# One wait slot per pair of column blocks and per token half, instead of one per block, in a six-layer transformer kernel on one Trainium2 core

## The reference

```python
for i in range(DEPTH):                       # 4 layers
    h = mixer_a / mixer_b / mixer_c (x)      # qkv = x @ w_qkv; attention of 16 heads; @ w_o
    x = layer_norm(DN_ALPHA * x + h, ...)
    x = layer_norm(DN_ALPHA * x + swiglu(x, w_gate_up[i], w_down[i]), ...)
for layer in range(DEPTH_2):                 # 2 layers
    proj = rmsnorm(x) @ w_in[layer]
    y_a = chunked_spatial_gating(...)
    y_b = mamba2_mixer(...)                  # state space scan in chunks of 128
    y_c = diff_attention(...)                # 4 heads, two softmaxes each; rmsnorm of the output
    merged = g0 * (y_a @ w_branch_a) + g1 * (y_b @ w_branch_b) + g2 * (y_c @ w_branch_c)
    x = x + merged @ w_out[layer]
    up = causal_dwconv(rmsnorm(x) @ ffn_w_up, ...)
    x = x + (silu(gate) * val) @ ffn_w_down
```

## Time and profile before

| | |
|---|---|
| median of 3 runs | 2586.41 us (2585.18 to 2586.76) |
| the profiled execution | 2585.18 us, its span 2583.4 us |
| PE busy | 2454.9 us, 95% of the span |
| DVE, ACT, POOL busy | 1477.3, 1324.3, 480.9 us |
| TensorE clock granted, mean | 0.969 of full |
| the chain that ended last | PE 82%, DVE 8%, ACT 5%, issue 3% |
| moved from and to memory | 398.94 MB, 154 GB/s |

### The profile page before, as it was taken

One profiled execution on the slowest core, in us unless ns is written; L12 is line 12 of the kernel. 1 busy time (PEld: TensorE's weight loads), 2 busy tenths in 40 slices (PEclk: granted clock), 3 DMA queues, 4 the chain that ended last, 5 costly groups with the idle time before them and its releaser, 6 DMA issues.

```text
span 2583.4 us, 36889 instructions
## 1 busy us (share of the span) xinstructions
PE 2454.9 (95%) x15388; PEld 2162.7 (84%) x15388; DVE 1477.3 (57%) x2114; ACT 1324.3 (51%) x1974; POOL 480.9 (19%) x370
## 2 busy tenths in 40 slices
PE   7999999999899998999989989999999999899999
PEld 5689977777699776998769979889899898798898
DVE  5455454544654545555555456656676666566766
ACT  4454455554544555544445446546565565465654
POOL 3230041322400223101410001342100004421000
PEclk9799999999899999999889999999999989999999
DMA  6145543333355433554315544334445443344453
GB/s 243 49 176 183 184 158 114 115 115 130 114 194 182 164 132 132 193 186 175 132 66 196 183 160 156 126 143 147 166 176 182 179 155 123 132 156 169 165 194 131
DMA packets 58182, 398.94 MB, mean 154 GB/s; under 512 B 6816, under 2 KB 7072, under 8 KB 11680
## 3 DMA queue, kind: packets, MB, share of 16 engines
q1 hardware_dynamic: 56864, 393.75, 41.9%
q10 hardware_dynamic: 1152, 2.83, 0.3%
HBM read 395.51 MB, written 1.05 MB: 154 GB/s over the span
## 4 chain that ended last, share of the span: by engine, by line
PE 82%; DVE 8%; ACT 5%; issue 3%; POOL 1%; DMA 0%; SPq 0%; DVEq 0%; ACTq 0%; POOLq 0%
PE b L1139 12%; PE b L1141 12%; PE b L1140 12%; PE b L1073 12%; PE b L1074 11%; PE b L1075 11%; PE b L1078 8%; PE b L1082 4%; DVE wlo L1780 2%; ACT whi L1415 2%; DVE xl L1792 1%; ACT full L1411 1%; DVE st L1843 1%; DVE xn L1841 1%; DVE xn L1854 0%
## 5 line engine op out<-in xcount | busy, mean ns | idle before, releaser
L1780 DVE TENSOR_TENSOR wlo<-raw,whi 128x2048 fp32r<-128x2048 f32 x351 | 823.0, 2348 | 441.6 <-ACT whi L1415 441.4
L1415 ACT ACTIVATE whi<-raw 128x2048 fp32r<-128x2048 f32 x362 | 690.8, 1910 | 356.4 <-PE b L1141 225.6
L1139 PE MATMUL b<-xh,whi 128*128 128x256 f32 x2560 | 728.7, 285 | 0.0
L1141 PE MATMUL b<-xh,wlo 128*128 128x256 f32 x2560 | 722.8, 282 | 0.0
L1140 PE MATMUL b<-xl,whi 128*128 128x256 f32 x2560 | 722.8, 282 | 0.0
L1139 PEld LDWEIGHTS b<-xh,whi 128*128 128x128 f32 x2560 | 486.5, 190 | 8.1 <-issue 6.1
L1140 PEld LDWEIGHTS b<-xl,whi 128*128 128x128 f32 x2560 | 486.7, 190 | 1.9
L1141 PEld LDWEIGHTS b<-xh,wlo 128*128 128x128 f32 x2560 | 486.2, 190 | 0.0
L1073 PE MATMUL b<-whi,xh 128*128 128x512 f32 x832 | 356.0, 428 | 54.4 <-issue 38.0
L1074 PE MATMUL b<-wlo,xh 128*128 128x512 f32 x832 | 337.3, 405 | 0.0
L1075 PE MATMUL b<-whi,xl 128*128 128x512 f32 x832 | 336.8, 405 | 0.0
(11 more groups left out here) (225 smaller groups left out, 2896.3 us busy)
## 6 DMA issues: line engine op xcount, KB each, us to landing
raw<-in_w SPq DMA_DIRECT2D x362, 1024.0 KB, 4.8
gt<-in_rows SPq DMA_DIRECT2D x8, 512.0 KB, 3.9
bt<-in_rows SPq DMA_DIRECT2D x8, 512.0 KB, 4.8
abq<-in_rows ACTq DMA_DIRECT2D x2, 768.0 KB, 4.7
x<-in_x SPq DMA_DIRECT2D x1, 1024.0 KB, 6.3
bc<-in_rows SPq DMA_DIRECT2D x4, 256.0 KB, 5.0
out<-x SPq DMA_DIRECT2D x4, 256.0 KB, 2.1
msk<-in_masks SPq DMA_DIRECT2D x1, 768.0 KB, 7.8
```

Source lines behind the costliest of these rows:

```text
L1139: pe.matmul(out, wh[:, k, cs], ah[:, kk, :], start=kk == 0 and s == 0, stop=False, skip_group_check=True)
L1141: last = pe.matmul(out, wl[:, k, cs], ah[:, kk, :], start=False, stop=final and k == 3, skip_group_check=True)
L1415: return ac.activation(out, i, ACT.Copy)
L1780: ve.tensor_tensor(B.wlo[s][:, :], B.raw[r][:, :], B.whi[s][:, :], ALU.subtract).then_inc(sem["loV"], 1)
```

## The change

In `col_out` the inner loop over the two column blocks of a pair and its yield are gone: one `col` step now emits both blocks (24 matmuls), and there is one yield behind it. In `row_acc` (the branch without a boundary) the yield moves out of the loop over k: one yield per token half. A `col` tile and a `row` tile now have two yields in place of four. `tok_out` and the boundary branch are as before. The number of matmuls, their order within a tile, and the semaphore counts are the same. 

```diff
--- before.py
+++ after.py
@@ -313,14 +313,13 @@
             w = self.tile(key)
             last = half == len(keys) - 1
             for i in range(2):
-                for s in range(2):
-                    self.step("col", g, half, i, s, w, src, pairs[i][s], last)
-                    if i and s:
-                        if last:
-                            self.gone_by_bank(w, ("col", g, 1))
-                        else:
-                            self.gone_by_count(w)
-                    yield
+                self.step("col", g, half, i, w, src, pairs[i], last)
+                if i:
+                    if last:
+                        self.gone_by_bank(w, ("col", g, 1))
+                    else:
+                        self.gone_by_count(w)
+                yield
             self.let_go(w)
 
     def row_acc(self, name, layer, blks, a, src, first, boundary=None):
@@ -335,9 +334,9 @@
                 for t in range(2):
                     for k in range(2):
                         self.step("row", a, blks[n], t, k, w, src, first and n == 0 and k == 0, t == k == 1)
-                        if t and k:
-                            self.gone_by_count(w)
-                        yield
+                    if t:
+                        self.gone_by_count(w)
+                    yield
                 self.let_go(w)
             return
         closed, between = boundary
@@ -1124,25 +1123,26 @@
                 b, n = use["opart", 4 + l, blk]
                 p.wait_ge(f"empty{b}", n + 1)
 
-    def col(g, half, i, s, w, src, block, final):
+    def col(g, half, i, w, src, pair, final):
         b, n = use["col", g, i]
         weight_ready(w)
         source_ready(src, half)
-        if half == s == 0:
+        if half == 0:
             p.wait_ge(f"empty{b}", n)
         wh, wl = B.cols_of(w)
         ah, al = (B.xh, B.xl) if src[0] == "x" else (B.oh, B.ol)
-        out = B.bank[b][:, 256 * s:256 * s + 256]
-        cs = slice(128 * block, 128 * block + 128)
-        for k in range(4):
-            kk = 4 * half + k
-            pe.matmul(out, wh[:, k, cs], ah[:, kk, :], start=kk == 0 and s == 0, stop=False, skip_group_check=True)
-            pe.matmul(out, wh[:, k, cs], al[:, kk, :], start=False, stop=False, skip_group_check=True)
-            last = pe.matmul(out, wl[:, k, cs], ah[:, kk, :], start=False, stop=final and k == 3,
-                             skip_group_check=True)
-        if s and final:
+        for s in range(2):
+            out = B.bank[b][:, 256 * s:256 * s + 256]
+            cs = slice(128 * pair[s], 128 * pair[s] + 128)
+            for k in range(4):
+                kk = 4 * half + k
+                pe.matmul(out, wh[:, k, cs], ah[:, kk, :], start=kk == 0 and s == 0, stop=False, skip_group_check=True)
+                pe.matmul(out, wh[:, k, cs], al[:, kk, :], start=False, stop=False, skip_group_check=True)
+                last = pe.matmul(out, wl[:, k, cs], ah[:, kk, :], start=False, stop=final and k == 3,
+                                 skip_group_check=True)
+        if final:
             last.then_inc(sem[f"full{b}"], 1)
-        elif s and i:
+        elif i:
             last.then_inc(sem["gone"], 1)
 
     def rows_ready(a, blk, src):
```

## The result

| | before | after |
|---|---|---|
| median | 2585.8 us (2581.97 to 2586.76) | 2647.8 us (2642.32 to 2649.34) |
| profiled execution | 2585.18 us, span 2583.4 | 2645.02 us, span 2643.1 |
| mean granted clock | 0.969 | 0.952 |

The change makes the kernel 2.4% slower: ratio 1.0239, 95% interval 1.0221 to 1.0256. The forecast was 2658 with a range of 2630 to 2690.

What follows compares the result with a forecast made beforehand. PE's own pace was taken to bound the feed-forward blocks and most projections. Terms 42 + 5 + 4 + 22 - 1.4 = 71.6 us on 2585.18 gave 2656.8; with the median 1.2 above, 2658 us, range 2630 to 2690.

Steps and rivals of the forecast that it cites:

- Term A: Layers 4 and 5, end of attention: PE waits before opart and ahead of the last pv, 21.0 us a layer, 42 us.
- the long one: Layers 4 and 5: PE waits for the whole chain between the last pv and opart, 16.9 us a layer.
- The shorter waits: Layers 4 and 5: PE idles ahead of the last pv while DVE copies the last probs, about 4.1 us a layer.
- Term B: Behind the wait before opart, layers 4 and 5: windows at half clock, 2.5 us a layer, 5 us, bounds 3 to 9.
- Term C: Layers 4 and 5: loV behind a score comes about 0.25 us late per head, 4 us, bounds 0 to 10.
- not slower: Rival: larger projection pieces cover attention's waits better and term A's chain is hidden; 2569 us, chance 0.02.
- Term D: Layers 0 to 3: attention without projection matmuls, waits and half clock, 22 us, bounds 0 and 49.
- Attention keeps the full clock: Rival, layers 0 to 3: bare attention costs only its 6 us of waits; 2642 us, chance 0.17.
- Half clock at once in all four layers: Rival, layers 0 to 3: attention falls to half clock at once, Term D is 49 us; 2685 us, chance 0.12.
- The feed-forward blocks at 0: Feed-forward blocks: moved activation steps cost 0, since PE waited for nothing there; same length within 1 us.

Runs made afterwards that it cites:

- e1: Kernel before with only the row_acc part of the change (one slot per token half, col tiles with four slots as before): 2611.56 us, 1.0096.
- e2: Kernel before with only the col_out part of the change (both blocks in one step, one slot behind them, row tiles as before): 2618.23 us, 1.0120.
- e3: Changed kernel with two yields in a row wherever the change has one, so as many slots as before: 2624.34 us, 1.0147.
- e7: Changed kernel with no loV recorded in drain() or in project's loop that waits for normalised rows: 2624.12 us, 1.0143.
- e12_turn: Kernel before with the rotation of a query tile's second half recorded 12 slots ahead of use, not 6: 2585.86 us, 0.9998.
- e10_early: Changed kernel with drain() ahead of both gates and the output projection behind them in layers 4 and 5: 2625.69 us, 1.0148.
- e14_mended: Changed kernel with no loV recorded while heads stand bare, drain() ahead of both gates and the output projection behind them: 2611.44 us, 1.0092.

## Why the prediction was right, and where its terms were off

**The mechanism** is the one forecast: fewer slots leave attention unplaced, and it then stands bare on PE. e1, e2 and e3 show it for layers 4 and 5 by number of slots. For layers 0 to 3 the loss comes with the `row` pieces alone (e1), and e7 shows that two thirds of it hang on the low halves recorded while the heads stand bare; e3 shows that giving the slots back in pairs does not cure it. The sum was 71.6 us on the profiled execution and 59.8 were measured, 12 us too much. Layers 4 and 5 were put 19 us too high and layers 0 to 3 6 us too low; in part the errors cancelled, which was luck.

**Term A** (42 us): its two waits are there, but the long one was over-sized, and this is the step that failed most. Forecast 16.9 us, measured 12.58. The working took two L2465 at their least of before, 1.68 us each, and left L2471 at 6.47 for two. Measured for these lines in the changed kernel (least, median, most):

```profile
L2465 POOL TENSOR_TENSOR og<-og,small x4: 1255/1448/1642, 1857.8 to 2392.2; 128x512 f32<-128x512 f32 x4
L2471 POOL TENSOR_SCALAR og<-og x4: 1488/1489/1489, 1860.8 to 2395.0; 128x512 f32<-128x512 f32 x4
```

With DVE idle, L2471 takes 2.94 for two, 3.5 us less than I put in, and L2465 0.5 less. I had applied the contention to one of the two POOL lines only. My reading of the earlier trace rows was half right too: the slow multiplications of the kernel before ran beside a `loV`, but the fast ones of 1.68 us ran beside DVE's products (`sigs<-b,sigs`, one input in PSUM), so products of that kind did not slow them. The shorter waits were forecast at 4.1 us and are 1.71 + 1.67 = 3.4. In all 16.0 us a layer against 21.0, so 32 us against 42.

**Term B** (5 us) holds about: 3.4 us at clock 0.50 with PE busy behind each wait, 1.7 us lost. The transposes take 1.97 us instead of 1.03. All that slower matmuls can have cost in both layers is the growth of PE's busy time, 4.6 us.

**Term C** (4 us) is not there: PE is busy for 49.00 of 49.00 us through the heads, and no wait for `wlo` of note appears. The 0.25 us were worked out from a margin (2.85 against 2.79) finer than what rows of merged instructions bear.

**Not forecast for layers 4 and 5:** the kernel before had waits in this stretch that now are gone. Ahead of L1139 it waited 3.9 us for a `wlo` of L1780, the changed kernel 1.0 us, and it waited 1.32 us for `og` ahead of one `pv` in each layer (1764.61 and 2283.71), which the 1.71 us of term A replace; against that a wait for `kT` grew in each layer from 0.83 to 2.39 us. That waits go where the pieces are larger is the effect that my rival "not slower" rested on; here it is small against the rest. By the table PE stands still for 27.5 us more, so of the 32 us of term A about 4.5 came back in this way. So 32 + 4.6 - 4.5 stand against the 32.2 us of the table, where I had 42 + 5 + 4 = 51.

**Term D** (22 us) was too small by a fifth: 27.9. It is the half clock, as forecast, not waits alone: PE stands still for 7.3 us more and is busy for 20.7 us more, with 157 us at the lower clock in place of 96. In layer 0: the wait of 3.54 us where the kernel before waits 0.92 in these heads; behind it 14.3 us of head work at half clock (114.53 to 130.53, less a wait of 1.73), which by 3.58 against 1.94 us a head costs some 6.5 us (an estimate); and the first seven projection matmuls, 3.13 us in place of some 1.6. That is 10.6 us against the 8.7 of the table; where the other 2 us came back I have not traced. The prediction took the waits from the earlier trace rows and named neither the `loV` in the chain nor the right place in the code. That was luck: the size came from two bounds far apart, of which I took near the middle. The Trainium skill, TensorE: Matmul & The Clock Gate, section Part 1: The HAM clock gate, says that the clock follows recent activity. The fall inside the 3.54 us wait (1.00 up to about 113.2 us, then 0.50) agrees. But that PE stays at 0.51 through 20.80 us in which its rows show it busy for 17.68, and holds 1.00 in the kernel before with 16.79, can't be told from the busy time of the rows, which is longer for the same matmul at half clock. e12_turn shows the same: taking a wait away did not keep the clock.

**The rivals.** *Attention keeps the full clock* gave 2642, nearer the measured 2647.8 than the forecast, but for the wrong reason: the clock did fall, and the error sat in terms A and C and in the waits that came back. *Half clock at once in all four layers* gave 2685: layers 1 and 2 lose 3.9 and 5.0 us, so no. The feed-forward blocks at 0 were right (-0.4 us for six).

What stays open: 9.7 us in layers 0 to 3 with e7_hold2, and 12.1 in layers 4 and 5 with e10_early. In the first PE stands still only 0.5 us longer than before and is busy for 9.3 us more, so it is mostly the lower clock, and no run shows what would keep it up. In the second it is 7.4 us of small waits and 4.6 us of longer busy time.

## What to carry to other kernels

- Before making pieces of work coarser for one engine, count what is left in the queue of side work when it is forced out. Then add up the chain of the other engines from the last forced step to the next use: here it was hidden by 42.9 us of weights and became a wait of 12.6 us, twice.
- Take each duration in that chain from a row with the neighbours that it will have. Here the two POOL steps of the exposed chain took 5.80 us, with VectorE idle, and 11.54 in cover.
- Where a background step is slipped in by count, look at which chain it lands in: here a 2.3 us step between a score and its softmax, which itself had to wait 1.5 us for its input, went with a wait of 3.5 us and then 20 us at half clock.

## What the runs showed of the hardware

- A GpSimd `tensor_scalar` of 128x512 with one tensor input took 1.49 us with VectorE idle (changed kernel and e2_cols, all four) and 2.75 to 3.42 us beside VectorE's `loV` with two inputs in SBUF (e10_early):

```profile
L2471 POOL TENSOR_SCALAR og<-og x4: 2752/3136/3422, 1855.8 to 2381.7; 128x512 f32<-128x512 f32 x4
```

- It goes both ways, and it matters what runs when an instruction begins. The first three rows are of the kernel before, the last of e10_early:

```profile
1787.80 2.28 DVE L1780 TENSOR_TENSOR wlo<-raw,whi 128x2048 fp32r<-128x2048 f32 x1
1787.79 3.43 POOL L2465 TENSOR_TENSOR og<-og,small 128x512 f32<-128x512 f32 x1
1789.99 3.38 DVE L1780 TENSOR_TENSOR wlo<-raw,whi 128x2048 fp32r<-128x2048 f32 x1
1858.41 2.29 DVE L1780 TENSOR_TENSOR wlo<-raw,whi 128x2048 fp32r<-128x2048 f32 x1 [0.53 <-ACT whi L1415]
```

  A `loV` and a multiplication began together. The `loV` took 2.28 us, its usual time (median 2.29), and the multiplication 3.43, which is 2.28 and 1.15 more; alone one took 1.26 us in the changed kernel. The next `loV` began 1.23 us before the end of that multiplication and took 1.10 us longer than usual. So the two durations look as if these instructions took turns; that is an inference from the rows, which no run tests by itself. A `loV` that began while a one-input `tensor_scalar` ran was held up little or not at all: 2.29 us in the last row, 2.69 us at 1835.29 in e14_mended.

  The Trainium skill, GPSIMD Engine Reference, section Key points, names two SBUF inputs of a VectorE instruction as a case of contention. The trace agrees, with these sizes.
